# The first block's residual: x read in 128-byte pieces and turned 32 by 32 on VectorE, in place of TensorE's transposes

## The chip, the cores and the metric

One NeuronCore of a Trainium2 chip runs the whole program. The metric is the device time of one execution in microseconds; lower is better. Engines named below: TensorE (PE), VectorE (DVE), ScalarE (ACT), GpSimd (POOL) and SyncE (SP, which here only issues DMAs).

## The reference, cut to what matters

Two blocks run one after the other on x of 512 tokens by 1024 features, all in float32. The first block's end is what this change touches:

```python
def first_block(x, ...):
        h = rmsnorm(x, norm_g[l])
        proj = h @ w_in[l]                      # q, k, v, za, u, vs, zs, gm
        a = (window_sink_attention(q, k, v) * silu(za)) @ w_att_out[l]
        sgo = (chunked_spatial_gating(gelu(u), gelu(vs)) * silu(zs)) @ w_sg_out[l]
        ga, gs = split(sigmoid(gm + b_merge[l]))
        y = ga * a + gs * sgo
        x = x + y @ w_o[l]                      # this x is the residual
    return rmsnorm(x, final_g)
```

The second block (gated convolution, pooling, a linear recurrence and an MLP) takes the result.

## The kernel before, in words

Activations are kept turned: 128 features on the partitions, eight chunks of features (`[:, k]`, k = 0 to 7), 512 tokens along the free dimension. The input x is tokens by features in memory, so whatever uses it in a sum with matmul results has to be turned first.

Weights come as blocks: one DMA of SP brings a block of 1 MB (1024 rows by 256 columns, so 1 KB pieces) into one of the two halves of `raw`. A block holds two tiles of 128 output columns. For each tile j, ScalarE rounds it to a high part in `whi` (`cast(j)`, L1033, recorded as L1031) and signals `hi`; GpSimd subtracts to get the low part in `wlo` (`low(j)`, L2524, four operations recorded at L2533) and signals `lo`. `whi` and `wlo` have three buffers each. TensorE's `product(j)` (L564, matmuls at L582) does 24 matmuls of 512 columns a tile: 16 with the high weights against the high and low activations, then 8 with the low weights. VectorE drains each product (L1640) and signals `drained`. Program order on every queue is written out by hand.

`load_block(blk)` (L426) waits until the last tile of block blk - 2 has its `lo`, since it overwrites that half of `raw`. The stretch that matters here has these tiles: 58 to 65 are the gate columns for the spatial gating branch (blocks 33 to 36, tile 62 and 63 in block 35, 64 and 65 in block 36), 66 to 73 multiply by w_sg_out (`J_SGO` = 66, blocks 37 to 40), 74 to 81 by w_o (`J_WO` = 74), whose drains add the residual.

SP's order around the change (L485 to L505): blocks 27 to 34; a wait for `small_zero` (VectorE has cleared the place of the small weights, after `gated` 3); six small loads of 256-byte pieces (L492, L496) and one of 256 KB (L498) into `P`; the load of x again into `F2` (L501, tokens on partitions, 4 KB pieces); then blocks 35 and on. `F2`'s 16 KB a partition are free once `gated` 3 is signalled.

ScalarE's order in that stretch (L1253 to L1265): for n = 0 to 7, `cast(60 + n)`; at n = 2 also the high part of the small weights (`small_high`, 1792 columns); then the sigmoid of gate n, which waits for the drain of tile 58 + n; then `copy(A8h[:, n])`. VectorE (L1951 to L1957): `gate_scaled(8 + n)`, which is the drain of tile 58 + n, then the low part of `A8`; after n = 1 the low part of the small weights (`small_low`), which waits for `small_high`.

The residual: TensorE's `x_again(k)` (L813) turns chunk k with four transposes (L818) into PSUM bank 4 or 5, once before tile 66 and once after each of tiles 66 to 72; ScalarE's `x_again(k)` (L1267) copies it to `F4[:, k]` and signals `x_again_set`. VectorE's drain of tile 74 + k (L2015) adds `F4[:, k]`.

Of the kernel before, what the change touches and what calls it, by code (L numbers as in the profile page):

```python
# [131 lines left out]
def build(nc, t):  # L132
    with ExitStack() as ctx:
        def sb(name, shape, dt=F32):
            return ctx.enter_context(nc.sbuf_tensor(name, shape, dt))

        b = Book(lambda name: ctx.enter_context(nc.semaphore(name)))
# [8 lines left out]
        ident = sb("ident", [128, 128])  # L146
# [19 lines left out]
        ps = ctx.enter_context(nc.psum_tensor("ps", [128, 8, 512], F32))  # L166
# [4 lines left out]
        F1f, F2f, F4f = (Fm[:, i, 0:4096] for i in range(3))  # L171
        F1, F2, F3, F4 = (F.rearrange("p (k n) -> p k n", k=8) for F in (F1f, F2f, F3f, F4f))
# [23 lines left out]
        x_v = t["x"][0].rearrange("(t p) c -> p t c", p=128)  # L196
# [47 lines left out]
        wpl = smallw[:, 1024:1280].rearrange("p (c n) -> p c n", c=2)  # L244
        wpw = smallw[:, 1280:1792].rearrange("p (c n) -> p c n", c=2)
        sh, sl = M[:, 0:1792], M[:, 1792:3584]
        xn2 = F2f.rearrange("p (t c) -> p t c", t=4)
        ss8 = ps[:, 7, 0:8]
        sq = [P[:, 512 * i:512 * i + 512] for i in range(4)]
        R1s = sq[3]  # L250
# [155 lines left out]
        def slot(u):  # L406
            return tmp[:, u % 7, 0:512]
# [17 lines left out]
        def sync_program(e, w):  # L425
# [12 lines left out]
            for n, (k0, k1) in enumerate(((0, 2), (2, 4), (4, 8))):  # L438
                c = slice(128 * k0, 128 * k1)
# [14 lines left out]
            for nm in ("final_g", "mix_norm_g_2", "mlp_norm_g_2", "final_norm_g_2", "b_merge", None, "pool_scale_2",  # L454
# [6 lines left out]
                n = src.shape[0] // 128  # L461
# [36 lines left out]
            e.dma_start(wpw, t["convb_pw_w_2"][0].rearrange("(c p) n -> p c n", p=128)).then_inc(  # L498
                *b.done("small_in", "all", 16))
            w.wait_ge("gated", 3)  # L500
            e.dma_start(xn2, x_v).then_inc(*b.done("x_again_in", 0, 16))  # L501

            first_up = len(blocks) - 16
            for blk in range(35, first_up):
# [58 lines left out]
        def tensor_program(e, w):  # L563
            def product(j, groups, xh, xl, x_ready, ks=range(8), free=(), start=True, stop=True, tail=0, between={}):  # L564

                w.wait_ge("hi", j)
                kk = blocks[tiles[j][0]][3]
                ks = list(ks)
                order = []
                for part in (ks[:len(ks) - tail], ks[len(ks) - tail:]):  # L570
                    order += [(k, w_hi, x) for k in part for x in (xh, xl)] + [(k, w_lo, xh) for k in part]
                for g, banks in enumerate(groups):
                    for ev in free[g:g + 1]:
                        w.wait_ge(*ev)
                    for n, (k, of, x) in enumerate(order):
                        if (g, n) in between:
                            between[g, n]()
                        w.wait_ge(*x_ready(k))
                        if of is w_lo:
                            w.wait_ge("lo", j)  # L580
                        for bk, c0, c1 in banks:
                            mm = e.matmul(ps[:, bk, 0:c1 - c0], of(j)[:, k % kk, 128 * g:128 * g + 128], x[:, k, c0:c1],  # L582
                                          start=(start and n == 0), stop=(stop and n == len(order) - 1))
                    mm.then_inc(*b.done("products", (j, g)))
# [87 lines left out]
            for j in range(J_Q, J_ZA):  # L672
                h_product(j, j % 3, [("drained", j - 3)] if j >= 3 else [],
                          {(0, 6): lambda: spread(3, "row")} if j == 2 else {})
                if j == 3:
                    w.wait_ge("drained", 1)
                    for i in range(4):
                        mm = e.transpose(ps[:, 6, 128 * i:128 * i + 128], slot(1)[:, 128 * i:128 * i + 128], ident[:])
# [115 lines left out]
            def rotating(j):  # L794
                return ROTATING[(j - J_GATE) % 4]

            for j in range(J_GATE, J_GS):
                n = j - J_GATE
# [11 lines left out]
            for j in range(J_GS, J_SGO):  # L810
                h_product(j, rotating(j), [("drained", j - 4)])

            def x_again(k):  # L813
                bk = 4 + k % 2
                w.wait_ge("x_again_in", 0)
                w.wait_ge(*(("x_again_set", k - 2) if k >= 2 else ("sg_v", (k, 0))))
                for i in range(4):
                    mm = e.transpose(ps[:, bk, 128 * i:128 * i + 128], xn2[:, i, 128 * k:128 * k + 128], ident[:])  # L818
                mm.then_inc(*b.done("x_again_turned", k))

            x_again(0)
            for n in range(8):
                j = J_SGO + n
                product(j, [[(rotating(j), 0, 512)]], A8h, A8l, lambda k: ("sg_low", k), free=[("drained", j - 4)])
                if n < 7:
                    x_again(n + 1)
            for j in range(J_WO, J_IN2):
                product(j, [[(rotating(j), 0, 512)]], Hh, Hl, lambda k: ("y_low", k), free=[("drained", j - 4)])

# [15 lines left out]
            def gate(c, a):  # L845
                xh, xl = gin[c]
                w.wait_ge("xc_low", c)
                w.wait_ge("small_low", 0)
                if (c, a) == (0, 0):
                    w.wait_ge("x_again_set", 7)  # L850
                else:
                    w.wait_ge("gates", (c, 0) if a else (c - 1, 1))
                for n, (m, x) in enumerate(((sh, xh), (sh, xl), (sl, xh))):
                    for h in range(2):
                        mm = e.matmul(ps[:, 4 + h, 0:264], m[:, 512 * a + 128 * c:512 * a + 128 * c + 128],
                                      x[:, 264 * h:264 * h + 264], start=(n == 0), stop=(n == 2))
                mm.then_inc(*b.done("gate_products", (c, a)))
# [157 lines left out]
            for r, c0, c1, bk in ((0, 0, 512, 6), (1, 0, 256, 7), (1, 256, 512, down_bank(3, P_5, 0))):  # L1015
                if bk < 4:
                    w.wait_ge("kept", (P_5, 0))
                for m, (k, of, x) in enumerate(order):
                    j = down_tile(3, P_4, k // 2)
                    w.wait_ge("hi", j)  # L1020
                    if of is w_lo:
                        w.wait_ge(*low_ready(j))
                    mm = e.matmul(ps[:, bk, 0:c1 - c0], x[:, k, 128 * r:128 * r + 128], of(j)[:, k % 2, c0:c1],  # L1023
                                  start=(m == 0 and bk < 4), stop=(m == 11))
# [4 lines left out]
        def scalar_program(e, w):  # L1029
            def copy(out, src, scale=1.0):  # L1030
                return e.activation(out, src, ACT.Copy, scale=scale)  # L1031
# [232 lines left out]
                w.wait_ge("products", (J_GS - 1, 0))  # L1264
                copy(A8h[:, n], F4[:, n]).then_inc(*b.done("sg_high", n))  # L1265

            def x_again(k):  # L1267
                w.wait_ge("x_again_turned", k)
                w.wait_ge("sg_low", k)
                copy(F4[:, k], ps[:, 4 + k % 2, :]).then_inc(*b.done("x_again_set", k))  # L1270

            x_again(0)
            w.wait_ge("decay_in", 0)
            e.activation(dk[1], dk[1], ACT.Exp).then_inc(*b.done("decay_exp", 0))
            for n in range(8):
                cast(68 + n)
                if n < 7:
                    x_again(n + 1)
                w.wait_ge("sg_added", n)
                w.wait_ge("products", (J_SGO - 1, 0))  # L1280
                copy(Hh[:, n], F1[:, n]).then_inc(*b.done("y_high", n))
# [350 lines left out]
        def vector_program(e, w):  # L1632
# [3 lines left out]
            def low(out, src, high):  # L1636
                return e.tensor_tensor(out, src, f(high), ALU.subtract)  # L1637
# [207 lines left out]
            for j in range(J_U, J_V):  # L1845
                k = j - J_U
# [112 lines left out]
            def decay():  # L1959

                a = dk
                e.tensor_scalar(a[0], lam, -1.0, None, ALU.mult).then_inc(*step())
                w.wait_ge("vector_step")
                e.tensor_tensor(a[1], lam, a[0], ALU.min).then_inc(*b.done("decay_in", 0))
                w.wait_ge("decay_exp", 0)
                e.tensor_scalar(a[2], a[1], 2.0, None, ALU.add).then_inc(*step())
                w.wait_ge("vector_step")
                e.reciprocal(a[2], a[2]).then_inc(*step())
                w.wait_ge("vector_step")
                e.tensor_tensor(a[1], a[1], a[2], ALU.mult).then_inc(*step())  # L1970
                w.wait_ge("vector_step")
                e.tensor_tensor(a[2], a[1], a[1], ALU.mult).then_inc(*step())
                w.wait_ge("vector_step")
                e.tensor_scalar(a[3], a[2], 1.0 / 17, 1.0 / 15, ALU.mult, ALU.add).then_inc(*step())
                for d in (13, 11, 9, 7, 5, 3, 1):
                    w.wait_ge("vector_step")
                    e.tensor_tensor(a[3], a[3], a[2], ALU.mult).then_inc(*step())
                    w.wait_ge("vector_step")
                    e.tensor_scalar(a[3], a[3], 1.0 / d, None, ALU.add).then_inc(*step())
                w.wait_ge("vector_step")  # L1980
                e.tensor_tensor(a[3], a[3], a[1], ALU.mult).then_inc(*step())
                e.tensor_scalar(a[0], a[0], 0.0, None, ALU.max).then_inc(*step())
                w.wait_ge("vector_step")
                e.scalar_tensor_tensor(a[3], a[3], 2.0, a[0], ALU.mult, ALU.add).then_inc(*step())
                w.wait_ge("vector_step")
                e.tensor_scalar(a[4], a[3], -8.0, None, ALU.mult)
                e.tensor_scalar(a[5], a[3], 8.0, None, ALU.mult).then_inc(*b.done("decay", 0))

            decay()
            for n in range(8):  # L1990
                j = J_SGO + n
                w.wait_ge("products", (j, 0))
                w.wait_ge("gs_gate", n)
                w.wait_ge(*slot_free(U_SGO + n))
                scaled(slot(U_SGO + n), ROTATING[n % 4], F3[:, n], j)
                w.wait_ge("drained", j)
                e.tensor_tensor(F1[:, n], F1[:, n], slot(U_SGO + n), ALU.add).then_inc(*b.done("sg_added", n))
                w.wait_ge("y_high", n)
                low(Hl[:, n], F1[:, n], Hh[:, n]).then_inc(*b.done("y_low", n))


            e.tensor_tensor(fm, g_f, g_m, ALU.mult).then_inc(*b.done("fm_set", 0))
# [729 lines left out]
```

## Time and profile before

| | us |
|---|---|
| median of 3 runs | 993.95 (993.51 to 994.23) |
| the profiled execution's own time | 993.99 |
| its span, first to last instruction | 992.2 |
| TensorE busy | 981.9 (99%) |
| ScalarE busy | 475.4 (48%) |
| VectorE busy | 622.8 (63%) |
| GpSimd busy | 526.0 (53%) |
| mean granted TensorE clock | 0.996 |

Some 1.8 us of the execution lie outside the span. A busy microsecond of TensorE is a modelled one (matmuls overlap), so its pace is read from the distance between the starts of the same instruction in successive tiles, not from its busy share.

### The profile page before, as it was taken

The numbers are of one execution on the slowest core, as the hardware profiler recorded it, in microseconds if no ns is written. First come the engines' busy times: TensorE is split into PE (matmuls) and PEld (weight loads), VectorE is DVE, ScalarE is ACT, GpSimd is POOL, SyncE is SP. The second block draws the span as 40 slices with busy tenths as digits, with TensorE's granted clock in tenths as the row PEclk, the third lists the DMA queues.
The fourth block names the chain that finished last, engine by engine and source line by source line (L and its number), as shares of the span: only waits on it lengthen the run. The fifth ranks groups of instructions, "written<-read, shape, count | busy, mean of one in ns | idle before, by whom it ended". The sixth has DMA issues, their size and how long they took to land.

```text
span 992.2 us, 12731 instructions
## 1 busy us (share of the span) xinstructions
PE 981.9 (99%) x4859; PEld 831.1 (84%) x4859; DVE 622.8 (63%) x930; ACT 475.4 (48%) x753; POOL 526.0 (53%) x625
## 2 busy tenths in 40 slices
PE   9999999999999999999999999999999999999996
PEld 7888888888888888888899988888888888888885
DVE  5782257665283752463669999874973681595697
ACT  4553455554672222543334866463644352453465
POOL 4555555565555884654656778565056027008212
PEclk9999999999999999999999999999999999999999
DMA  7323221212453225332223123277657347536347
GB/s 236 115 74 116 85 86 56 73 43 80 117 176 95 86 85 194 102 106 90 64 85 106 44 68 125 86 268 179 167 170 185 113 149 179 143 84 192 60 77 178
DMA packets 93196, 117.49 MB, mean 118 GB/s; under 512 B 4002, under 2 KB 70080, under 8 KB 93136
## 3 DMA queue, kind: packets, MB, share of 16 engines
q1 hardware_dynamic: 86384, 102.20, 31.9%
q0 software_dynamic: 6448, 14.16, 8.3%
q8 instruction: 38, 0.62, 0.3%
q10 hardware_dynamic: 304, 0.33, 0.1%
q14 instruction: 22, 0.18, 0.1%
HBM read 110.91 MB, written 2.10 MB: 114 GB/s over the span
## 4 chain that ended last, share of the span: by engine, by line
PE 93%; DVE 5%; issue 1%; ACT 1%; ACTq 0%; DVEq 0%
PE ps L582 64%; PE ps L977 15%; PE ps L601 4%; PE ps L727 1%; DVE ps L2091 1%; PE ps L651 1%; PE ps L748 1%; PE ps L712 1%; PE ps L711 1%; PE ps L789 1%; DVE Hl L1637 0%; DVE tmp L2135 0%; PE ps L627 0%; PE ps L1023 0%; PE ps L634 0%
## 5 line engine op out<-in xcount | busy, mean ns | idle before, releaser
L2533 POOL TENSOR_TENSOR wlo<-raw,whi 128x256 fp32r<-128x256 f32 x496 | 401.4, 862 | 221.3 <-ACT whi L1031 221.2
L582 PE MATMUL ps<-Hh,whi 128*128 128x512 f32 x512 | 202.5, 395 | 0.0
L582 PE MATMUL ps<-Hl,whi 128*128 128x512 f32 x512 | 200.3, 391 | 0.0
L1031 ACT ACTIVATE whi<-raw 128x1024 fp32r<-128x1024 f32 (+1 forms) x126 | 132.3, 1050 | 95.5 <-PE ps L582 54.7
L582 PE MATMUL ps<-Ah,whi 128*128 128x512 f32 (+1 forms) x496 | 165.2, 359 | 0.0
L582 PE MATMUL ps<-Al,whi 128*128 128x512 f32 (+1 forms) x496 | 163.6, 356 | 0.0
L582 PE MATMUL ps<-Hh,wlo 128*128 128x512 f32 x512 | 129.7, 390 | 0.0
L582 PEld LDWEIGHTS ps<-Hh,whi 128*128 128x128 f32 x512 | 96.7, 189 | 19.8
L582 PEld LDWEIGHTS ps<-Hl,whi 128*128 128x128 f32 x512 | 96.8, 189 | 19.5
L582 PEld LDWEIGHTS ps<-Hh,wlo 128*128 128x128 f32 x512 | 96.1, 188 | 20.0
L582 PE MATMUL ps<-Ah,wlo 128*128 128x512 f32 (+1 forms) x496 | 104.8, 356 | 0.0
L582 PEld LDWEIGHTS ps<-Ah,whi 128*128 128x128 f32 x496 | 88.0, 188 | 13.0
L582 PEld LDWEIGHTS ps<-Al,whi 128*128 128x128 f32 x496 | 88.0, 188 | 12.8
L582 PEld LDWEIGHTS ps<-Ah,wlo 128*128 128x128 f32 x496 | 83.3, 188 | 13.3
L2574 POOL DMA_DIRECT2D w_w<-in_w_down x16 | 19.5, 1216 | 119.0 <-DVE wlo L1637 51.4
L2321 DVE SCALAR_TENSOR_TENSOR X<-ps,Rb 128x512 f32<-128x512 f32 x32 | 21.8, 689 | 87.0 <-PE ps L582 86.2
L2544 POOL TENSOR_TENSOR P<-P,sm 128x1024 f32<-128x1024 f32 (+1 forms) x16 | 26.9, 1680 | 52.0 <-DVE sm L1830 52.0
L977 PE MATMUL ps<-whi,Hl 128*128 128x512 f32 x216 | 53.3, 389 | 0.0
L1640 DVE TENSOR_TENSOR tmp<-ps,Rb 128x512 f32<-128x512 f32 x25 | 17.2, 689 | 53.8 <-PE ps L582 53.8
L582 PE MATMUL ps<-Ah,w_more 128*128 128x512 f32 x160 | 50.2, 389 | 0.0
L977 PEld LDWEIGHTS ps<-whi,Hl 128*128 128x128 f32 x216 | 40.5, 188 | 8.4
L2533 POOL TENSOR_TENSOR w_more<-raw,w_more 128x256 fp32r<-128x256 f32 x40 | 30.9, 931 | 19.4 <-ACT w_more L1031 19.4
(373 smaller groups left out, 1670.0 us busy)
## 6 DMA issues: line engine op xcount, KB each, us to landing
raw<-in_w_in SPq DMA_DIRECT2D x29, 1024.0 KB, 5.3
raw<-in_w_up SPq DMA_DIRECT2D x16, 1024.0 KB, 5.5
Fm<-in_w_down SPq DMA_DIRECT2D x8, 1024.0 KB, 5.0
w_w<-in_w_down POOLq DMA_DIRECT2D x16, 512.0 KB, 5.8
raw<-in_w_in SPq DMA_DIRECT2D x14, 512.0 KB, 3.7
raw<-in_w_att_out SPq DMA_DIRECT2D x4, 1024.0 KB, 5.1
raw<-in_w_sg_out SPq DMA_DIRECT2D x4, 1024.0 KB, 5.3
raw<-in_w_o SPq DMA_DIRECT2D x4, 1024.0 KB, 5.1
```

The lines of the kernel that those rows point to most:

```text
L582: mm = e.matmul(ps[:, bk, 0:c1 - c0], of(j)[:, k % kk, 128 * g:128 * g + 128], x[:, k, c0:c1], start=(start and n == 0), stop=(stop and n ...
L601: mm = e.matmul(ps[:, banks[r], :], x[:, k, 128 * r:128 * r + 128], of(j)[:, k % 2], start=(i == 0 and n == 0), stop=(i == 3 and n == 5))
L651: mm = e.matmul(ps[:, i, :], of(i)[:, k], x[:, k], start=(k == 0 and of is w_hi and x is Hh), stop=last)
L711: e.matmul(out, lhs, kdh[:, g, k0:k0 + W], start=True, stop=False)
L712: mm = e.matmul(out, lhs, kdl[:, g, k0:k0 + W], start=False, stop=True)
L977: mm = e.matmul(ps[:, down_bank(part, n, r), :], x[:, k, 128 * r:128 * r + 128], of(j)[:, k % 2], start=(first and fresh), stop=(last and ...
L1031: return e.activation(out, src, ACT.Copy, scale=scale)
L1640: e.tensor_tensor(out, ps[:, bk, :], R, ALU.mult).then_inc(*b.done("drained", j))
L2321: e.scalar_tensor_tensor(X[:, n], ps[:, up_bank(part, n), :], 0.0, RB, ALU.max, ALU.mult).then_inc(*b.done("drained", j))
L2533: ins = e.tensor_tensor(w_lo(j)[:, *cut], raw_tile(j)[:, *cut], f(w_hi(j))[:, *cut], ALU.subtract)
L2544: e.tensor_tensor(Pf[:, u, :, :, 0:W], Pf[:, u, :, :, 0:W], rb, ALU.mult).then_inc(*b.done("probs", i))
L2574: e.dma_start(w_sum3[h] if n == P_7 else quarter(0, 1, h), src, accum_op=ALU.add).then_inc(*b.done(w_sum_name(n, h), (part, n), 16))
```

## The change

x is read a second time by four DMAs of 512 KB, one for each group of 32 partitions. Partition 32c + r receives, for every chunk k and every q = 0 to 15, the 32 features 128k + 32c to 128k + 32c + 31 of token 32q + r: 128 contiguous bytes of memory. Each DMA so consists of 32 x 8 x 16 = 4096 pieces of 128 bytes, 16384 in all, where before there were 512 pieces of 4 KB. VectorE then transposes each 32 by 32 square in place of its grid (one instruction of 128 x 512 for a chunk), which gives features on partitions and tokens along the free dimension, straight into `F4[:, k]`. TensorE's 32 transposes, ScalarE's eight copies, and the waits on them go. The eight new instructions of VectorE stand one behind each `y_low(n)` in the loop over tiles 66 to 73.

```diff
-        xn2 = F2f.rearrange("p (t c) -> p t c", t=4)
+        x_blocks = F2f.rearrange("p (k q f) -> p k q f", k=8, q=16)
+        x_b = t["x"][0].rearrange("(q r) (k c f) -> c r k q f", r=32, c=4, f=32)
...
             w.wait_ge("gated", 3)
-            e.dma_start(xn2, x_v).then_inc(*b.done("x_again_in", 0, 16))
+            for c in range(4):
+                e.dma_start(x_blocks[32 * c:32 * c + 32], x_b[c]).then_inc(*b.done("x_again_in", c, 16))
...
-            def x_again(k):
-                bk = 4 + k % 2
-                w.wait_ge("x_again_in", 0)
-                w.wait_ge(*(("x_again_set", k - 2) if k >= 2 else ("sg_v", (k, 0))))
-                for i in range(4):
-                    mm = e.transpose(ps[:, bk, 128 * i:128 * i + 128], xn2[:, i, 128 * k:128 * k + 128], ident[:])
-                mm.then_inc(*b.done("x_again_turned", k))
-            x_again(0)
             for n in range(8):
                 j = J_SGO + n
                 product(j, ...)
-                if n < 7:
-                    x_again(n + 1)
...
-                if (c, a) == (0, 0):
-                    w.wait_ge("x_again_set", 7)
-                else:
+                if (c, a) != (0, 0):
                     w.wait_ge("gates", (c, 0) if a else (c - 1, 1))
...
-            def x_again(k):          # ScalarE
-                w.wait_ge("x_again_turned", k)
-                w.wait_ge("sg_low", k)
-                copy(F4[:, k], ps[:, 4 + k % 2, :]).then_inc(*b.done("x_again_set", k))
...
+            def x_again(k):          # VectorE
+                w.wait_ge("x_again_in", 3)
+                w.wait_ge("sg_low", k)
+                e.transpose(F4[:, k], F2f[:, 512 * k:512 * k + 512]).then_inc(*b.done("x_again_set", k))
...
                 low(Hl[:, n], F1[:, n], Hh[:, n]).then_inc(*b.done("y_low", n))
+                x_again(n)
```

## Rows read from the trace of the kernel before

**Rows 1.** The page, chain that ended last: share of the span by engine.

```profile
PE 93%; DVE 5%; issue 1%; ACT 1%; ACTq 0%; DVEq 0%
```

**Rows 2.** Waits of TensorE over the span: who, for whom, us, times, longest.

```profile
PE ps L634 <- DVE ones L1643: 1.2, 1, 1.2
PE ps L870 <- DVE tmp L2244: 0.5, 1, 0.5
```

**Rows 3.** Timeline of TensorE, tiles 61 to 63: start us, us, operation.

```profile
391.27 0.39 PE L582 MATMUL ps<-Hh,whi 128*128 128x512 f32 x1
...
396.71 0.39 PE L582 MATMUL ps<-Hh,whi 128*128 128x512 f32 x1
...
402.15 0.39 PE L582 MATMUL ps<-Hh,whi 128*128 128x512 f32 x1
```

**Rows 4.** Timeline of TensorE beside the transposes (L818).

```profile
418.47 0.60 PE L818 MATMUL ps<-ident,Fm 128*128 128x128 f32 x4
...
424.39 0.60 PE L818 MATMUL ps<-ident,Fm 128*128 128x128 f32 x4
...
459.93 0.60 PE L818 MATMUL ps<-ident,Fm 128*128 128x128 f32 x4
```

**Rows 5.** Timeline of SP's queue: start us, us, DMA issued.

```profile
381.91 0.46 SPq L501 DMA_DIRECT2D Fm<-in_x  x1
382.41 4.40 SPq L431 DMA_DIRECT2D raw<-in_w_in  x2
```

**Rows 6.** DMA issues: KB each, median us from issue to landing.

```profile
Fm<-in_x SPq DMA_DIRECT2D x1, 2048.0 KB, 8.1
```

**Rows 7.** DMA queues, 382.3 to 394.6 us: packets, MB, share of 16 engines.

```profile
q1 hardware_dynamic: 2736, 4.31, 102.8%
```

**Rows 8.** The same, 380 to 380.5 us: one load in 256-byte pieces.

```profile
q1 hardware_dynamic: 263, 0.06, 55.9%
```

**Rows 9.** The same, 489 to 491.7 us: one load in 512-byte pieces.

```profile
q1 hardware_dynamic: 1035, 0.52, 66.9%
```

**Rows 10.** The same, 17.0 to 17.3 us: 64-byte pieces of `att_sinks`.

```profile
q1 hardware_dynamic: 21, 0.00, 4.6%
```

**Rows 11.** Timeline of ScalarE, 392 to 403 us.

```profile
393.02 1.06 ACT L1031 ACTIVATE whi<-raw 128x1024 fp32r<-128x1024 f32 x1 [5.02 <-DMA raw<-in_w_in]
393.98 1.69 ACT L1031 ACTIVATE M<-P 128x1792 fp32r<-128x1792 f32 x1
398.81 0.72 ACT L1261 ACTIVATE F<-tmp,vec 128x512 f32<-128x512 f32 x1 [3.14 <-DVE tmp L1640]
399.44 0.61 ACT L1031 ACTIVATE Ah<-Fm 128x512 fp32r<-128x512 f32 x1
399.95 1.05 ACT L1031 ACTIVATE whi<-raw 128x1024 fp32r<-128x1024 f32 x1
```

**Rows 12.** Timeline of VectorE, same stretch.

```profile
395.70 2.47 DVE L1637 TENSOR_TENSOR M<-P,M 128x1792 fp32r<-128x1792 f32 x1 [6.98 <-ACT M L1031]
398.09 0.68 DVE L1640 TENSOR_TENSOR tmp<-ps,Rb 128x512 f32<-128x512 f32 x1
```

**Rows 13.** Timeline of GpSimd, same stretch.

```profile
394.16 4.62 POOL L2533 TENSOR_TENSOR wlo<-raw,whi 128x256 fp32r<-128x256 f32 x4 [7.75 <-ACT whi L1031]
```

**Rows 14.** Windows of 1 us: busy us of each engine, PEclk, DMA share, GB/s.

```profile
625.00:626.00 1.00, 1.00 (x5) 0.86 (x6) 0.97 (x4) 0.00 (x0) 1.00 (x2) 0.72 0.00 0
...
628.00:629.00 1.00, 1.00 (x4) 0.79 (x3) 0.35 (x1) 0.97 (x3) 1.00 (x2) 0.57 0.87 258
...
984.00:985.00 1.00, 0.29 (x3) 0.09 (x1) 0.86 (x5) 0.48 (x3) 0.00 (x0) 1.00 0.00 0
...
987.00:988.00 1.00, 0.00 (x0) 0.00 (x0) 0.64 (x1) 0.52 (x2) 0.00 (x0) 0.63 0.54 199
```

**Rows 15.** VectorE: a shuffle of one tile, and idle time before its drains, 418 to 475 us.

```profile
L1701 DVE STREAM_SHUFFLE ps<-ps x9: 686/689/694, 25.8 to 70.8; 128x512 f32<-128x512 f32 x9
...
L1640 DVE TENSOR_TENSOR tmp<-ps,F 128x512 f32<-128x512 f32 x8 | 5.5, 690 | 16.0 <-PE ps L582 16.0
```

More of the change, by code:

```diff
@@ L1265, in scalar_program @@
                 copy(A8h[:, n], F4[:, n]).then_inc(*b.done("sg_high", n))
-            def x_again(k):
-                w.wait_ge("x_again_turned", k)
-                w.wait_ge("sg_low", k)
-                copy(F4[:, k], ps[:, 4 + k % 2, :]).then_inc(*b.done("x_again_set", k))
-            x_again(0)
             w.wait_ge("decay_in", 0)
@@ L1276, in scalar_program @@
                 cast(68 + n)
-                if n < 7:
-                    x_again(n + 1)
                 w.wait_ge("sg_added", n)
```

## The prediction

> **What bounds the kernel now.** I read the page first, then TensorE's waits, then the stretch around the second load of x on every engine. The chain that ended last runs over TensorE for 93% of the span [rows 1], and the waits of TensorE over the whole span are few and short, the longest 1.2 us at the very start [rows 2]. So TensorE's own instructions set the time, one after another, and what they need is nearly always there before them. A change pays if it takes instructions off TensorE, and costs if it makes something arrive late. Outside the transposes a tile takes 5.44 us from start to start [rows 3].
>
> Where is the slack smallest near the change? SP issues x again at 381.91 us and block 35 right behind it, at 382.41 [rows 5]. ScalarE's `cast(62)`, the first tile of that block, then starts at 393.02 after 5.0 us of idleness that the DMA of the block ended [rows 11]. TensorE needs tile 62 at 396.71 and tile 63 at 402.15 [rows 3]. That is a queue where the x load stands directly ahead of a weight block that arrives just in time.
>
> **What goes: TensorE's transposes.** Between the first and the eighth group of four lie 459.93 - 418.47 = 41.46 us for seven tiles, 5.92 us each [rows 4]; without a group it is 5.44. A group so costs 0.48 us, and eight of them 3.86 us. All of it is on the path. ScalarE loses eight copies of a chunk and gains nothing for the path, since it idles here anyway.
>
> **What comes on VectorE: eight transposes of 128 x 512.** The trace has none. The nearest row is the shuffle of such a tile at 0.69 us [rows 15], which moves data between partitions too. Bounds: 0.69 us below, and above three times that, 2.1 us, if four-byte squares take several passes; I take 0.69. In the loop over the eight tiles VectorE idles 16.0 us before its drains, 2.0 us a tile [rows 15], so 5.5 us more in all is hidden, and even 2.1 us each would make a drain late by only 0.1 us. Only the last matters to TensorE: tile 74 needs `y_low(7)`, and `x_again(7)` stands behind that. `x_again(6)` stands ahead of the drain of tile 73, in its idle time. Queued behind `x_again(7)` are the small steps for the meta tokens and the drain of tile 74, a whole tile later. I cost it at nothing, up to 0.5 us if it were 2.1 us each.
>
> The new wait, `x_again_in` 3, comes first at the transpose behind `y_low(0)`, after 430 us, when the load has had almost 50 us. Under none of the prices below does it hold.
>
> **What changes in the queue: the load of x.** Before, 2.10 MB in 4 KB pieces. Over 382.3 to 394.6 us the queue moved 4.31 MB, the last 256 KB of the small weights, x and blocks 35 and 36, without a pause, at 351 GB/s [rows 7]. x's share of it is 2.10 / 4.31 x 12.3 = 6.0 us of all 16 engines (8.1 us from issue to landing [rows 6]). Now it is 16384 pieces of 128 bytes, 1024 for each engine. What does one cost? No row shows this size, but its neighbours are there, each as share x 16 x window / packets:
> - 64 bytes: 4.6% x 16 x 0.3 us / 21 = 10.5 ns [rows 10]
> - 256 bytes: 55.9% x 16 x 0.5 us / 263 = 17.0 ns [rows 8]
> - 512 bytes: 66.9% x 16 x 2.7 us / 1035 = 27.9 ns [rows 9]
>
> The line between 64 and 256 bytes gives 12.7 ns at 128, the price of the larger neighbour 17.0. The neighbours are bursts of at most 64 pieces an engine; here 1024 come in a row, each 32 rows (128 KB of memory) from the last, and written into 32 partitions at a time. I therefore take the middle of the upper part, 14.8 ns: 1024 x 14.8 ns = 15.2 us. From below the bound is half of the 256-byte price, 8.5 ns (8.7 us); from above the pace of a whole 256-byte load with its start and end, 0.5 us for 263 pieces or 1.90 ns each over all engines [rows 8]: 31.1 us. The three further issues of SP, some 0.46 us each [rows 5], run while the first of the four loads is being moved.
>
> One rule speaks for a cheaper piece. The Trainium skill, "DMA: Bandwidth & Descriptors", section "Why small descriptors are slow (HBM only)", has a fixed part of 3 cycles beside one cycle for 32 bytes, 11 cycles for 256 bytes and so 7 for 128. The rows agree in kind (double the bytes, 1.6 times the time, from 256 to 512); with it the 17.0 ns would become an estimated 10.8 ns, the load 11.1 us, and the kernel 994.3 us.
>
> **From the load to TensorE.** The queue's loads land in the order of issue (x at 381.9 + 8.1 = 390.0, block 35 at 393.0 [rows 5, 6, 11]), so I let block 35 land later by the growth of x: D = 15.2 - 6.0 = 9.2 us. From its landing a series runs without a gap: `cast(62)` (393.02 to 394.08), the high part of the small weights to 395.67 [rows 11], their low part on VectorE to 398.17 and the drain of tile 60 behind it [rows 12], then on ScalarE sigmoid, copy and `cast(63)`, ready at 401.00 [rows 11]. TensorE wants tile 63 at 402.15 [rows 3]: the slack is 1.15 us, less than tile 62's own (396.71 - 394.08 = 2.63 us) and less than that of its low part (ready 398.78 [rows 13], wanted 16/24 of a tile after 396.71, at 400.34: 1.56 us). The smallest decides: TensorE falls behind by D - 1.15 = 8.05 us.
>
> During this it stands still from 396.71 to 394.08 + 9.2 = 403.3, 6.6 us. At the end of the kernel the granted clock fell to 0.5, which is 1.2 GHz, some 3 us after the last matmul; a spell of half clock elsewhere lasted from 625.4 to 628.9 [rows 14]. So it will fall here, and 3.4 us at half speed cost 1.7 us. Tile 62 then takes 5.44 + 1.7 = 7.1 us, but tile 63 is not ready before 401.00 - 394.08 = 6.9 us after tile 62 anyway: 0.2 us is all that it adds. Block 36 lands 2 to 3 us behind 35 and is wanted 5.4 us after tile 63; block 37 waits for `lo` of tile 63 and shifts with it. TensorE has no slack later in which to win anything back.
>
> **Sum**, against the profiled 993.99 us (the median of the runs is 0.04 lower, nothing): + 8.05 + 0.2 - 3.86 = + 4.4 us, 998.4 us.
>
> **Rivals.**
> 1. The pieces are cheap, and the change comes out even. At the 64-byte price, 10.5 ns: 10.8 us, D = 4.8, TensorE 3.6 us late, 993.7 us. The second way to it: 32 partitions take half of the rate of 128, 175 GB/s [rows 7], 12.0 us, D = 6.0, 4.85 us late, 995.0 us. For it the steady fall of price with size; against it the scattered source. The Trainium skill, "SBUF — State Buffer", section "Door 1: The DMA port swizzle", says that partitions 0 to 31 reach 8 of 16 ports and gives 189 GB/s for them at 1 MiB; by it the load would take an estimated 11.1 us and the kernel 994.3 us, and no row here shows a load into 32 partitions.
> 2. Faster. The delay stays under the slack plus what the transposes gave: at 8.5 ns, D = 2.7, 1.55 us late, 991.7 us; wholly hidden (D under 1.15, a load of up to 7.1 us), 990.1 us. By the sum above the change is the load's time less 11.0 us, so it decides from 9.0 us down (8.8 ns a piece). Against it: it needs a price under that of 64 bytes. It would also come if block 35 were moved beside x and not behind it, for which nothing in the trace speaks.
> 3. Far slower: the engines are not the limit but the making of pieces, or the memory behind addresses 128 KB apart. At 31.1 us D = 25.1, 24.0 us late, 1014.3 us; halfway, 23 us, it is 1006.0.
> 4. The transposes of VectorE cost more than I think and hold up its drains: even at 2.1 us each 0.5 us, so no case of its own.
>
> **Chances.** Forecast (load of 13 to 19 us) 0.50; rival 1 (9 to 13) 0.21; rival 2 0.10; rival 3 0.19. A measurement of this kernel tells about 0.2%, 2 us, from no change: slower needs a load of over 13 us (0.69), same lies between 9 and 13 (0.21), faster below (0.10). The range takes in rival 1 and most of rival 3: 992.0 to 1009.0; the forecast's own is 996 to 1002.
>
> **What would show it.** L818 gone and the tiles 66 to 73 at 5.44 us: + 3.86. DMA engines busy for some 15 us over 16384 packets from 382 us at about 140 GB/s. `cast(62)` at 402 us, released by the DMA, and TensorE with one hole of 6 to 7 us before tile 62 and PEclk at 0.5 behind it. VectorE's transposes at 0.7 us with no wait for the DMA. I am wrong if the load lands within 9 us, if the hole is not there, or if a second hole stands at a later block or at tile 74.

## The result: slower by 0.15%, a third of what was forecast

The changed kernel takes 995.04 us (median of 22 runs, 994.31 to 997.22), the kernel before 993.95 us (22 runs). The ratio is 1.0015, 95% interval 1.0009 to 1.0022: 1.5 us slower (the two medians lie 1.1 us apart). Nine of the 22 runs took 995.7 to 997.2 us and the others 994.3 to 995.1, as did the traced one (994.77); one run of four_loads, further down, took 4635 us at a granted clock of 0.20 and is left out of its ratio. Its profiled span is 993.0 us, before it was 992.2. Forecast were + 4.4 us and 998.4. The direction holds, and the queue, the hole and the half clock are found as they were written down; the cost was put too high.

The page of the changed kernel, busy time by engine and the chain that ended last, against [rows 1]:

```profile
PE 978.7 (99%) x4827; PEld 828.2 (83%) x4827; DVE 630.4 (63%) x938; ACT 471.4 (47%) x745; POOL 527.4 (53%) x625
...
PE 88%; DVE 6%; ACT 2%; DMA 1%; SPq 1%; issue 1%; ACTq 0%; DVEq 0%
```

TensorE's share of the chain has fallen from 93% to 88%: SP's queue (SPq), the DMA of a weight block and more of ScalarE now stand in it. All of that is one place. SP's queue there, against [rows 5] (start, us, what is issued):

```profile
381.40 0.60 SPq L500 DMA_DIRECT2D P<-in_convb_pw_w  x1
382.05 9.01 SPq L504 DMA_DIRECT2D Fm<-in_x  x4
391.10 3.47 SPq L433 DMA_DIRECT2D raw<-in_w_in  x2
```

The x load, 0.46 us of SP's time before, holds SP for 9 us, 2.6 to 2.9 for each of the last three, and block 35 is issued at 391.10 and not at 382.41. ScalarE's row of `cast(62)` and of `cast(63)`, against [rows 11]:

```profile
399.20 1.06 ACT L1021 ACTIVATE whi<-raw 128x1024 fp32r<-128x1024 f32 x1 [11.07 <-DMA raw<-in_w_in]
400.16 1.68 ACT L1021 ACTIVATE M<-P 128x1792 fp32r<-128x1792 f32 x1
...
406.11 1.05 ACT L1021 ACTIVATE whi<-raw 128x1024 fp32r<-128x1024 f32 x1
```

The prediction calls D the time by which block 35 lands later; it is read here from the issue of x to `cast(62)`. `cast(62)` starts 399.20 - 382.05 = 17.15 us after the issue of x; before it was 393.02 - 381.91 = 11.11. D is 6.04 us. From there to `cast(63)` it is 6.91 us, before 6.93: the series is what it was. TensorE, against [rows 3] (the last low matmuls of tile 61, the first matmul of 62, one of its middle, the first of 63):

```profile
395.02 1.97 PE L585 MATMUL ps<-Hh,wlo 128*128 128x512 f32 x8
400.31 0.50 PE L585 MATMUL ps<-Hh,whi 128*128 128x512 f32 x1 [3.31 <-ACT whi L1021]
...
402.24 0.63 PE L585 MATMUL ps<-Hl,whi 128*128 128x512 f32 x1
...
407.47 0.39 PE L585 MATMUL ps<-Hh,whi 128*128 128x512 f32 x1
```

The hole is 3.3 us. Tile 62 starts at 400.31 and tile 63 at 407.47, 7.16 us for a tile. Everything in this execution lies 0.14 us later than in the one before (x is issued at 382.05, not 381.91), so tile 63 is late by 407.47 - 402.15 - 0.14 = 5.18 us. The granted clock and the DMA engines, windows of 1 us (columns as in [rows 14]):

```profile
385.00:386.00 1.00, 1.00 (x6) 0.81 (x6) 0.00 (x0) 0.00 (x0) 1.00 (x3) 1.00 1.38 218
386.00:387.00 1.00, 1.00 (x6) 0.84 (x5) 0.69 (x1) 0.12 (x1) 0.54 (x1) 1.00 0.89 139
...
389.00:390.00 1.00, 1.00 (x6) 0.84 (x5) 0.00 (x0) 0.00 (x0) 0.00 (x0) 1.00 0.97 152
...
394.00:395.00 1.00, 1.00 (x6) 0.82 (x5) 0.00 (x0) 0.00 (x0) 0.00 (x0) 1.00 0.91 155
...
398.00:399.00 1.00, 0.00 (x0) 0.00 (x0) 0.00 (x0) 0.00 (x0) 0.00 (x0) 1.00 1.08 360
...
402.00:403.00 1.00, 1.00 (x4) 0.81 (x3) 1.00 (x1) 0.00 (x0) 1.00 (x2) 0.50 0.00 0
```

Three things are to be seen. Small pieces run at 218 GB/s with a DMA share of 1.38. In 386 and 389 the rate drops, where one of the four loads ends and the next begins. And TensorE's clock is at 0.5 in 402, as forecast, after a hole of 3.3 us where 6.6 was forecast.

The transposes of VectorE, of which before had no row:

```profile
L1975 DVE STREAM_TRANSPOSE Fm<-Fm x8: 699/703/705, 436.7 to 470.3; 128x512 f32<-128x512 f32 x8
```

0.70 us each, and no wait for the load. Without TensorE's transposes tiles 66 to 73 take 5.44 us each.

One thing must be known before the two traces are compared as wholes. Here is a short wait of TensorE that both have, in the kernel before and in the changed one, and below it the low matmuls of one and the same tile, again before and after:

```profile
622.80 1.05 PE L870 MATMUL ps<-ones,tmp 128*128 128x1 f32 x8 [0.53 <-DVE tmp L2244]
624.27 0.94 PE L860 MATMUL ps<-ones,tmp 128*128 128x1 f32 x7 [0.53 <-DVE tmp L2233]
```

```profile
662.56 1.98 PE L582 MATMUL ps<-Ah,wlo 128*128 128x512 f32 x8
662.83 1.98 PE L585 MATMUL ps<-Ah,wlo 128*128 128x512 f32 x8
```

At 623 us the changed kernel is late by 1.47 us, 1.33 without the shift of 0.14: just the 5.18 lost less the 3.86 of the transposes. At 663 it is late by 0.27 only. Between them lies the spell of half clock from 625.4 to 628.9 [rows 14], which the changed kernel's execution doesn't have: the clock is 1.00 there. It cost the kernel before 1.2 us, so that the two traced executions lie only 0.8 us apart (994.77 and 993.99; some 0.5 of that comes after the last matmul, which starts at 984.17 and 983.89). The spell is not tied to the change: late_before, cost_alone and pieces_128p below have it, late_again, gain_alone, four_again and two_loads do not. What decides it, and whether it makes the two groups of run times, was not found out.

### The profile page after: what moved, and what is told of

The parts are those of the page before. It is cut to its first block, busy times and chain, and to the rows that moved or that the text cites. A ratio compares the mean times of both kernels' runs of the same rounds, so it can differ in the third digit from the quotient of the medians.

```text
span 993.0 us, 12663 instructions
## 1 busy us (share of the span) xinstructions
PE 978.7 (99%) x4827; PEld 828.2 (83%) x4827; DVE 630.4 (63%) x938; ACT 471.4 (47%) x745; POOL 527.4 (53%) x625
## 4 chain that ended last, share of the span: by engine, by line
PE 88%; DVE 6%; ACT 2%; DMA 1%; SPq 1%; issue 1%; ACTq 0%; DVEq 0%
PE ps L585 62%; PE ps L967 14%; PE ps L604 4%; PE ps L730 1%; DVE ps L2080 1%; PE ps L654 1%; PE ps L751 1%; SPq L504 1%; DMA raw<-in_w_in 1%; PE ps L715 1%; PE ps L714 1%; DMA Fm<-P 1%; ACT whi L1021 1%; PE ps L792 1%; DVE Hl L1619 0%
```

## The experiments

First the account: is the loss only the place in the queue, and the gain only TensorE's transposes?

**late_load and late_again**, the same kernel twice: the changed kernel with the four loads behind block 36.

```diff
-            for c in range(4):
-                e.dma_start(x_blocks[32 * c:32 * c + 32], x_b[c]).then_inc(*b.done("x_again_in", c, 16))
...
             for blk in range(35, first_up):
                 load_block(blk)
+                if blk == 36:
+                    for c in range(4):
+                        e.dma_start(x_blocks[32 * c:32 * c + 32], x_b[c]).then_inc(*b.done("x_again_in", c, 16))
```

> The changed kernel with its four loads of x issued behind weight block 36 and not ahead of block 35; nothing else differs. Theory 1 (the whole loss is that block 35 stands behind the slower load): block 35 lands some 6 us after its issue again, TensorE has no hole, and the 3.9 us of the transposes stay: about 990.1 us, 3.9 us under the kernel before. Rival (the loss lies elsewhere, in the scattered load slowing the weights wherever it stands, or in VectorE's transposes): the load only moves the hole to block 36 or 37, and the time stays at 994 to 996 us.

> The changed kernel with its four loads of x behind block 36 once more, for a closer ratio to the kernel before and to the changed kernel: 990.1 to 990.4 us, 3.7 us under the kernel before, with every load of x in the gap of the queue before block 37.

Measured: 990.35 us, ratio 0.9960 (0.9947 to 0.9972), and 989.92 us, ratio 0.9960 (0.9948 to 0.9973). That is 4.0 us under the kernel before and better than both kernels. In the trace of late_again, SP's queue, ScalarE's `cast(62)` and `cast(63)`, and the longest of TensorE's waits:

```profile
382.54 4.80 SPq L433 DMA_DIRECT2D raw<-in_w_in  x2
387.39 12.02 SPq L509 DMA_DIRECT2D Fm<-in_x  x4
399.46 2.62 SPq L433 DMA_DIRECT2D raw<-in_w_sg_out  x1
```

```profile
388.45 1.04 ACT L1022 ACTIVATE whi<-raw 128x1024 fp32r<-128x1024 f32 x1
...
395.37 1.05 ACT L1022 ACTIVATE whi<-raw 128x1024 fp32r<-128x1024 f32 x1
```

```profile
PE ps L638 <- DVE ones L1626: 1.2, 1, 1.2
```

The loads still hold SP for 12 us, until 399.46, but now `cast(62)` runs at 388.45 and nobody waits for what stands behind them; TensorE's longest wait in the whole span is the one at the start. The rival, a hole that only moves on, falls. TensorE reaches the wait that stood at 622.80 in the kernel before at 619.46, and everything in this execution lies 0.57 us later (the load ahead of block 35 is issued at 381.82, where its like before was at 381.25): 3.91 us won up to there, for the 3.86 forecast.

**late_before**: the kernel before with its one load behind block 36, same edit.

> The kernel before with its one load of x (4 KB pieces, 128 partitions) issued behind block 36; nothing else differs. Both theories: TensorE did not wait there, so the place of the load gives nothing: 994.0 us, the same. If it came out faster, the gain of the moved load in the changed kernel would be partly the place and not the transposes.

Measured: 993.87 us, ratio 0.9998 (0.9989 to 1.0007). The place alone gives nothing, so late_load's gain is that of the changed transposes.

**gain_alone**: the changed kernel, x loaded as before; the residual is in the wrong order.

```diff
-            for c in range(4):
-                e.dma_start(x_blocks[32 * c:32 * c + 32], x_b[c]).then_inc(*b.done("x_again_in", c, 16))
+            e.dma_start(F2f.rearrange("p (t c) -> p t c", t=4), x_v).then_inc(*b.done("x_again_in", 3, 16))
```

> The changed kernel with x loaded as before (one load, 4 KB pieces, 128 partitions, ahead of block 35); VectorE transposes what then lies there, so the residual is in the wrong order. It is the gain alone. Theory 1: TensorE has no hole, eight groups of transposes at 0.48 us are gone: 3.9 us faster, 990.1 us. Rival (VectorE's eight transposes cost something near tile 74): 991 to 992 us.

Measured: 989.75 us, ratio 0.9955 (0.9942 to 0.9967), 4.5 us faster. 3.9 lies within the interval (3.3 to 5.8 us); the traced execution is one without the spell at 625 us.

**cost_alone**: the kernel before with the four loads; the residual is wrong.

```diff
-            e.dma_start(xn2, x_v).then_inc(*b.done("x_again_in", 0, 16))
+            for c in range(4):
+                e.dma_start(x_blocks[32 * c:32 * c + 32], x_b[c]).then_inc(*b.done("x_again_in", c, 16))
...
-                w.wait_ge("x_again_in", 0)
+                w.wait_ge("x_again_in", 3)
```

> The kernel before with the four loads of 128-byte pieces in place of its one load; TensorE still does its 32 transposes, on what then lies there, so the residual is wrong. It is the cost alone. Theory 1: tile 62 starts some 3.5 us late, tile 63 some 5.2 us late, and nothing is won back: 999.2 us, 5.2 us slower. Rival (part of the hole is made good later, or the changed kernel loses elsewhere): 996 to 998 us.

Measured: 1000.47 us, ratio 1.0059 (1.0046 to 1.0071), 5.9 us slower. The halves add up: - 4.5 + 5.9 = + 1.4, and the whole change is + 1.5. Each half is uncertain by some 1.2 us, so that they agree to 0.1 is luck.

Then the rate: what limits the load to 218 GB/s, the 32 partitions or the small pieces? Both were in my sum.

**four_loads and four_again**, the same kernel twice: the kernel before with four loads of 32 partitions in 4 KB pieces.

```diff
-            e.dma_start(xn2, x_v).then_inc(*b.done("x_again_in", 0, 16))
+            for c in range(4):
+                e.dma_start(xn2[32 * c:32 * c + 32], x_v[32 * c:32 * c + 32]).then_inc(*b.done("x_again_in", c, 16))
...
-                w.wait_ge("x_again_in", 0)
+                w.wait_ge("x_again_in", 3)
```

> The kernel before with its load of x cut into four loads of 32 partitions, still in 4 KB pieces; the result is the same. Port theory (what limits the changed load is that each of its loads writes only 32 partitions): 218 GB/s here too, 2.10 MB in 9.6 us and more, block 35 lands 3.6 to 5 us late, TensorE loses 2.5 to 4 us: 996.5 to 998 us. Piece theory (the 128-byte pieces are the limit, 9.4 ns each on each engine): 4 KB pieces run at 350 to 400 GB/s as before, 994.0 us, the same.

> The kernel before with its load of x cut into four loads of 32 partitions in 4 KB pieces, once more, now for its trace: it was some 3.3 us slower. Port theory, for large pieces: each load runs at some 218 GB/s or less, and block 35 lands 3.5 to 5 us late. Rival (the large pieces run at 350 GB/s and more, and the time goes into the gaps between the loads): short bursts at full rate with pauses between.

Measured: 997.46 us, ratio 1.0033 (1.0021 to 1.0045), and 997.31 us, 1.0033 (1.0017 to 1.0048), 3.3 us slower. The trace of four_again, a window in the middle of the loads and `cast(62)`:

```profile
388.00:389.00 1.00, 1.00 (x6) 0.83 (x5) 0.00 (x0) 1.00 (x2) 0.00 (x0) 1.00 1.01 209
```

```profile
398.73 1.06 ACT L1032 ACTIVATE whi<-raw 128x1024 fp32r<-128x1024 f32 x1 [9.57 <-DMA raw<-in_w_in]
```

Large pieces that ran at 404 GB/s into 128 partitions (385 to 388 us of the kernel before) run at some 210 into 32. x was issued at 383.06, so D = 15.67 - 11.11 = 4.56 us, less the 1.15 of slack 3.4: the measured 3.3.

**two_loads**: the same with two loads of 64 partitions.

> The kernel before with its load of x cut into two loads of 64 partitions in 4 KB pieces; the result is the same. Port theory: 64 partitions are no better than 32, about 218 GB/s, block 35 lands 3.5 us late, 996 to 997 us. Rivals: 64 partitions take twice the rate of 32 and the full one, 994.0 us; or only the gaps between loads cost, one in place of three, 995 us.

Measured: 998.78 us, ratio 1.0050 (1.0034 to 1.0067). Its window:

```profile
388.00:389.00 1.00, 1.00 (x6) 0.81 (x6) 0.00 (x0) 1.00 (x2) 0.00 (x0) 1.00 1.03 209
```

64 partitions are no faster than 32 (212 and 213 GB/s over 387 to 394 and 386 to 394 us), as the port theory has it. The Trainium skill, "SBUF — State Buffer", section "Door 1: The DMA port swizzle", states just that; these two runs agree. The time was forecast at 996 to 997 us and came out above it: the trace has x issued at 383.00 and `cast(62)` at 398.78, so D = 4.67 and a loss of 3.5 us, and four runs gave 5.0 (3.4 to 6.7). The rest was not found.

**pieces_128p**: small pieces, but each of the four loads writes all partitions (wrong order).

```diff
-        x_b = t["x"][0].rearrange("(q r) (k c f) -> c r k q f", r=32, c=4, f=32)
+        x_b = t["x"][0].rearrange("(n a) (b c f) -> c (a b) n f", n=32, c=4, f=32)
...
-                e.dma_start(x_blocks[32 * c:32 * c + 32], x_b[c]).then_inc(*b.done("x_again_in", c, 16))
+                e.dma_start(F2f[:, 1024 * c:1024 * c + 1024].rearrange("p (n f) -> p n f", f=32), x_b[c]).then_inc(
+                    *b.done("x_again_in", c, 16))
```

> The changed kernel with four loads of 4096 pieces of 128 bytes each again, but every load writes all 128 partitions (32 pieces a partition, 64 KB apart in memory where the changed kernel's are 128 KB apart), so the residual is in the wrong order. Port theory: the loads run faster than 218 GB/s, at 280 or more, x is through in 7 to 8 us, TensorE loses 0 to 1 us: 990.5 to 991.5 us. Piece theory, and the theory that SP makes pieces no faster (4096 in 2.7 us): 218 GB/s or less again, 995 us as the changed kernel.

Measured: 995.66 us, ratio 1.0016 (1.0007 to 1.0025), as the changed kernel.

```profile
385.00:386.00 1.00, 1.00 (x6) 0.81 (x6) 0.00 (x0) 0.00 (x0) 1.00 (x2) 1.00 1.38 218
```

Still 218. The port theory, which four_loads bore out for large pieces, fails as the sole reason here. x is issued at 382.50 and `cast(62)` starts at 399.14, D = 5.53, 0.5 us less than in the changed kernel (one trace of each).

**one_load_128p**: one load of all 16384 pieces (`"(q r) (g k f) -> (r g) k q f"`, r=32, g=4, f=32; wrong order).

> The changed kernel with one load of 16384 pieces of 128 bytes, into all 128 partitions, pieces 128 KB apart in memory; the residual is in the wrong order. It takes away the three gaps between the four loads (the rate fell to some 100 GB/s or less for a few tenths of a us each) and the port limit together. Port theory: 280 GB/s or more, no gaps, 990 to 991 us. Piece theory: 218 GB/s without gaps, 9.6 us in place of 11.4, 993 us.

Measured: 994.00 us, ratio 1.0001 (0.9992 to 1.0010). Two of its windows and its issue-to-landing time:

```profile
385.00:386.00 1.00, 1.00 (x6) 0.84 (x5) 0.00 (x0) 0.00 (x0) 1.00 (x3) 1.00 1.38 217
...
390.00:391.00 1.00, 1.00 (x6) 0.85 (x5) 0.00 (x0) 0.00 (x0) 0.00 (x0) 1.00 1.38 218
```

```profile
Fm<-in_x SPq DMA_DIRECT2D x1, 2048.0 KB, 12.0
```

The rate is 217 to 218 without a break. `cast(62)` (at 398.01, x issued at 381.98) came 16.03 us after the issue, D = 4.92 and not 6.04. Of these 1.1 us some 0.6 go with the three gaps (5.53 in pieces_128p, four loads into all partitions, against 4.92) and 0.5 with the 32 partitions of each load. The port theory's number is missed by 3 us, the piece theory's by 1.

**two_queues**: partitions 0 to 63 on SP's queue, 64 to 127 on ScalarE's at the same time.

```diff
-            for c in range(4):
+            for c in range(2):
...
+                if n == 1:
+                    w.wait_ge("gated", 3)
+                    for c in (2, 3):
+                        e.dma_start(x_blocks[32 * c:32 * c + 32], x_b[c]).then_inc(*b.done("x_more_in", c, 16))
                 cast(60 + n)
...
-                w.wait_ge("x_again_in", 3)
+                w.wait_ge("x_again_in", 1)
+                w.wait_ge("x_more_in", 3)
```

> The changed kernel with the loads of partitions 0 to 63 on SP's queue as now, and those of partitions 64 to 127 on ScalarE's queue at the same moment (just ahead of its cast of tile 61, which has 8 us of slack); the result is the same. Port theory: the two halves of the partitions don't share ports, so the rate goes above 218 GB/s, to 300 or more: x through in about 7 us, 990.5 to 991.5 us. Piece theory: the same 16 engines pay 9.4 ns a piece, 218 GB/s and at best the gaps filled: 993 to 995 us.

Measured: 994.66 us, ratio 1.0006 (0.9997 to 1.0014).

```profile
387.00:388.00 1.00, 1.00 (x6) 0.83 (x5) 0.00 (x0) 1.00 (x2) 1.00 (x2) 1.00 1.38 217
```

Two queues that write both halves of the partitions at once get the same 217 GB/s; only the gaps are filled (`cast(62)` at 398.10, x issued at 381.98: D = 5.01).

**pieces_near**: 128-byte pieces 256 bytes apart in memory, two loads into all partitions (wrong order; `"(p s) (b a f) -> a p (s b) f"`, s=4, a=2, f=32).

> The changed kernel with x in 16384 pieces of 128 bytes that lie only 256 bytes apart in memory (two loads of 8192 pieces into all 128 partitions); the residual is in the wrong order. Piece theory: the same 218 GB/s as with pieces 128 KB apart, 994 to 994.6 us. Rival (the memory behind the scattered pieces is the limit): faster than 218 GB/s, 991 to 993 us.

Measured: 995.36 us, ratio 1.0014 (1.0005 to 1.0023), 0.8 us above the piece theory's range.

```profile
387.00:388.00 1.00, 1.00 (x6) 0.81 (x6) 0.10 (x1) 0.87 (x2) 0.00 (x0) 1.00 1.38 218
```

218 again. Pieces 256 bytes apart run at the rate of pieces 64 KB (pieces_128p) and 128 KB apart; the scatter costs nothing in rate.

**pieces_256, pieces_512, pieces_1k**: one load into all partitions, pieces 128 KB apart, of 256 bytes, 512 bytes and 1 KB (f = 64, 128, 256; wrong order).

> The changed kernel with one load of x in 8192 pieces of 256 bytes into all 128 partitions, 128 KB apart in memory; the residual is in the wrong order. It prices the next size by its pace. Piece theory with a fixed part (128 bytes at 9.4 ns on each engine, 1 KB at some 47): about 14 to 15 ns, 280 to 290 GB/s, x through in 7.5 us: 991 us. A price that depends on the number of pieces alone (9.4 ns): the full rate, 350 GB/s and more, 990.2 us. The price I took from the trace before, 17.0 ns: 241 GB/s, 8.7 us, 991.8 us.

> The changed kernel with one load of x in 4096 pieces of 512 bytes (32 a partition, all 128 partitions, 128 KB apart in memory); the residual is in the wrong order. So far 128 and 256 bytes both settled at 218 GB/s, while weight blocks in 512-byte pieces (8 a partition) reach 348 in this kernel. Size theory (pieces of 256 bytes and less are capped at 218, larger ones not): 340 GB/s, 990.2 us. Depth theory (what caps is that every engine fills one partition for long, so that all sit on half of the ports at a time): 218 GB/s again, 993 us.

> The same with 2048 pieces of 1 KB, 16 a partition, 128 KB apart; the residual is in the wrong order. Size theory: 350 GB/s and more, 990 us. Depth theory: near 218 GB/s, 993 us, though the load of 4 KB pieces (4 a partition) runs at 400.

Measured: 992.96, 991.73 and 989.73 us, ratios 0.9989 (0.9980 to 0.9999), 0.9979 (0.9969 to 0.9988) and 0.9958 (0.9945 to 0.9972). Their windows, 256 bytes early and late, then 512 bytes early and late, then 1 KB:

```profile
385.00:386.00 1.00, 1.00 (x6) 0.81 (x6) 0.00 (x0) 0.00 (x0) 1.00 (x3) 1.00 1.29 272
...
390.00:391.00 1.00, 1.00 (x6) 0.82 (x5) 0.00 (x0) 0.00 (x0) 0.00 (x0) 1.00 1.35 218
```

```profile
385.00:386.00 1.00, 1.00 (x6) 0.81 (x6) 0.00 (x0) 0.00 (x0) 1.00 (x3) 1.00 1.09 327
...
389.00:390.00 1.00, 1.00 (x6) 0.84 (x5) 0.00 (x0) 0.00 (x0) 0.00 (x0) 1.00 1.19 289
```

```profile
388.00:389.00 1.00, 1.00 (x6) 0.82 (x5) 0.36 (x1) 0.61 (x2) 0.00 (x0) 1.00 1.10 356
```

256-byte pieces begin at 272 GB/s and settle at 218, the rate of 128 bytes, so 9.4 ns is no fixed price of a piece; my expectation of 280 to 290 was neared for some 1 us only, and none of the three times forecast (991, 990.2 and 991.8 us) was met. 512 bytes begin at 327 and settle at 290, between the size theory's 340 and the depth theory's 218; 1 KB runs at 350. Beside them stood the forecast's other candidate: by the fixed part of 3 cycles that the Trainium skill gives ("DMA: Bandwidth & Descriptors", section "Why small descriptors are slow (HBM only)") 256 bytes would run an estimated 1.27 times as fast as 128; here both settle at 218 GB/s, and the measurement decides.

**eight_256**: 256-byte pieces in eight loads, 8 pieces a partition and load (wrong order).

> The changed kernel with x in eight loads of 1024 pieces of 256 bytes each, 8 a partition and load, all 128 partitions; the residual is in the wrong order. Size theory: no window above 218 GB/s for long, with gaps between the loads, 993 us or more. Depth theory: each load runs at 270 GB/s or more, as the first 2 us of the single 256-byte load did; with SP's 0.65 us an issue x is through in about 8 us, 991 to 992 us.

Measured: ratio 0.9991 (0.9982 to 1.0000), 993.0 us.

```profile
384.00:385.00 1.00, 1.00 (x7) 0.81 (x6) 0.02 (x1) 0.25 (x1) 0.68 (x1) 1.00 1.10 285
385.00:386.00 1.00, 1.00 (x6) 0.84 (x5) 0.00 (x0) 0.00 (x0) 1.00 (x3) 1.00 1.23 263
...
390.00:391.00 1.00, 1.00 (x6) 0.84 (x5) 0.00 (x0) 0.00 (x0) 0.00 (x0) 1.00 1.33 223
```

It too starts high and settles near 218 (the window at 384 still holds 98 larger packets of the load ahead; the one at 385, all of 256 bytes, has 263), with 8 pieces a partition and load as with 64: the number of pieces that a partition gets in a row is not the reason. What makes 218 the level for small pieces into any partitions, and 212 to 213 the level for large ones into 32 or 64, stays open; that both come to about half of the full rate does not show that they are one limit.

## Why the prediction was right and wrong

**Right: what bounds, and where.** The load of x stood ahead of block 35, the block came later by the growth of the load, the series from its landing to `cast(63)` ran as priced (6.91 us for 6.92), the half clock behind the hole stretched tile 62 to 7.16 us for the 7.1 forecast. With D = 6.04 put into the same sum, 6.04 - 1.15 + 0.2 - 3.86 = + 1.2 us; TensorE in the trace is late by 1.33 at 623 us, and the runs gave + 1.5 (0.9 to 2.2).

**Right: the gain.** 3.86 us from the pitch [rows 4], 3.91 in the trace of late_again; the runs gave 4.0 in late_load and 4.5 in gain_alone, with 3.9 within both intervals. VectorE's transposes took 0.70 us for the 0.69 taken and were hidden.

**Wrong: the price of a piece.** The step that failed is "I therefore take the middle of the upper part, 14.8 ns: 1024 x 14.8 ns = 15.2 us". The pace in the changed kernel is 128 bytes x 16 / 218 GB/s = 9.4 ns, 9.6 us for the whole; with all that came on top the load cost what 12.0 us would in my account (D + 6.0). Two errors stand in the step, both shown. The first: the rows that I took the prices from give share x window / packets, and that is how long a packet lasts, not how often one ends. The same reading of the changed kernel:

```profile
DMA packets 1702, 0.22 MB, mean 218 GB/s; under 512 B 1702, under 2 KB 1702, under 8 KB 1702
...
q1 hardware_dynamic: 1702, 0.22, 138.3%
```

138.3% x 16 x 1 us / 1702 = 13.0 ns, while at a share of 1.38 packets overlap, and the engine ends one every 9.4 ns. My bursts had shares under 0.7 [rows 8 to 10], where nothing tells how far packets can overlap. That my line between the 64- and the 256-byte row had said 12.7 is luck, since a burst does not even give the length of a packet in a long load. The same row of pieces_256, 390 to 391 us:

```profile
q1 hardware_dynamic: 852, 0.22, 134.5%
```

134.5% x 16 x 1 us / 852 = 25.3 ns, where the burst of 256-byte pieces had 17.0 [rows 8]. The second error: I went up from 12.7 to 14.8 for scattered addresses, which pieces_near shows to cost nothing in rate, and for the 32 partitions, which by pieces_128p cost small pieces nothing in rate and some 0.5 us of D.

**Missed: the gaps and SP's time.** Each load of 4096 pieces behind another holds SP some 2.7 us, and the engines run low between two of them: with the 32 partitions 1.1 us of D by one_load_128p. I had written that the further issues run beside the first load. A further 1.3 us (D + 6.0 = 10.9 us in one_load_128p, against 9.6 at the pace) has two parts. I took x's old load at the mean rate of the queue, 351 GB/s and 6.0 us; x itself ran at 404, 5.2 us, which is 0.8 of it. The other 0.5 was not told apart. With the pace right and nothing else the sum would have been 9.6 - 11.0 = - 1.4 us, an error to the other side. So the price was 15.2 - 9.6 = 5.6 us too high and 2.4 us were left out; that the forecast missed by only 3 is partly luck.

**The rivals.** Rival 1 (cheap pieces or half the rate, 993.7 to 995.0 us, a load of 9 to 13 us) is the case that came, with 0.21. Its second way is the level that was measured for small pieces, though not its reason: all partitions give the same. Rival 3 had a chance of 0.19 for a limit in making pieces or in memory; no load came near its 23 or 31 us, but as it is open what sets 218 GB/s, a limit of that kind is not excluded as its reason.

## What to carry to other kernels

Before a load is made slower, look at what stands behind it in its queue and at how late that is allowed to land; moving the same four loads behind two weight blocks turned + 1.5 us into - 4.0. A DMA share times its window over its packets is the length of a packet; the pace needs a stretch in which the engines are full. A large load should span all partitions (four loads of 32 cost 3.3 us here), and pieces of 128 and of 256 bytes, once settled, cost alike by the byte. And two traces can differ by a spell of half clock that has nothing to do with the change: compare them up to the same instruction before it, and the run times beside that.

## What was not expected of the hardware

- Pieces of 128 and 256 bytes both settle at 217 to 218 GB/s, whatever the partitions, the distance in memory, the number of loads or of queues; 512 bytes settle at 290 in a long load; a weight load of 512 KB in such pieces, over in 2.7 us [rows 9], peaks at 348 (490.5 to 491 us).
- 256-byte pieces run at 263 to 272 GB/s in an early window and fall to 221 to 224 in the next, then to 218; 512-byte pieces run at 326 for 2 us and then fall to 290.
- Large pieces into 32 partitions and into 64 run at the same 212 to 213 GB/s.
- An issue of 4096 pieces keeps SP for 2.6 to 2.9 us when another load is ahead of it, and the following load starts into a gap.
- The granted clock fell to 0.5 behind a hole of 3.3 us in the changed kernel and behind one of 2.2 us in one_load_128p, and stayed at 1.00 behind one of 2.8 us in pieces_128p, where tile 62 then waited 0.8 us for its low part instead.
